# Two-block transformer kernel: halves at the four seams, six modulation sums from two-part accumulators, earlier division of attention's rows

## What is computed

```python
mod = c @ w_ada[l] + b_ada[l]          # first block; the second uses silu(c)
shift_m, scale_m, gate_m, shift_f, scale_f, gate_f = jnp.split(mod, 6, axis=-1)
h = modulate(rms_norm(x, g_pre_mix[l]), shift_m, scale_m)
y_a = sliding_window_attention(q_a, k_a, v_a, attn_sinks[l])
merged = sigmoid(g_a) * (y_a @ w_branch_attn[l]) + sigmoid(g_m) * (y_m @ w_branch_mlstm[l])
x = x + gate_m * rms_norm(merged @ w_out[l], g_post_mix[l])
h2 = modulate(rms_norm(x, g_pre_ffn[l]), shift_f, scale_f)
x = x + gate_f * rms_norm((silu(h2 @ w_gate) * (h2 @ w_up)) @ w_down, g_post_ffn[l])
# the second block: layer norms, a gMLP and an RWKV mixer, and a feed-forward of the same shape
```

## Time and profile before

| | |
|---|---|
| median of three runs | 795.09 us |
| profiled execution | 793.67 us |
| its span | 791.8 us, so 1.9 us lie around it |
| TensorE (PE) busy | 761.5 us, 96% |
| VectorE (DVE) busy | 615.4 us, 78% |
| ScalarE (ACT) busy | 375.9 us, 47% |
| chain that ended last | PE 71%, DVE 20%, DMA 4%, issue 3%, ACT 2% |
| read from HBM | 171.60 MB, 218 GB/s over the span |

### The profile page before, as it was taken

How to read it: one execution, slowest core, us unless ns; L and a number is a source line. 1 busy time by engine, 2 the same in 40 slices (tenths; PEclk the granted TensorE clock), 3 DMA queues, 4 the chain that set the end, 5 groups by cost and what they waited for, 6 DMA issues and landing times.

```text
span 791.8 us, 15369 instructions
## 1 busy us (share of the span) xinstructions
PE 761.5 (96%) x6380; PEld 675.7 (85%) x6380; DVE 615.4 (78%) x813; ACT 375.9 (47%) x553; POOL 41.4 (5%) x61
## 2 busy tenths in 40 slices
PE   4999999989999999999999999999899999999996
PEld 3798899989768999998876987989675999999874
DVE  5869989988978888887868899786697788556457
ACT  3367743744354544453345696432225444454340
POOL 0124000000000000000001000040010000000000
PEclk9999999999999999999999999999999999999998
DMA  9997867764668899988992644301673399666621
GB/s 342 319 318 223 296 213 221 246 227 129 199 230 309 291 351 322 343 303 302 371 334 61 204 128 138 108 4 46 202 236 105 114 315 319 187 189 199 195 83 53
DMA packets 98067, 173.65 MB, mean 219 GB/s; under 512 B 7767, under 2 KB 55230, under 8 KB 97998
## 3 DMA queue, kind: packets, MB, share of 16 engines
q1 hardware_dynamic: 95678, 166.62, 62.8%
q0 software_dynamic: 1872, 5.86, 2.6%
q10 hardware_dynamic: 448, 0.19, 0.1%
HBM read 171.60 MB, written 1.05 MB: 218 GB/s over the span
## 4 chain that ended last, share of the span: by engine, by line
PE 71%; DVE 20%; DMA 4%; issue 3%; ACT 2%; DVEq 0%; SPq 0%; ACTq 0%
PE bank L2246 12%; PE bank L2247 12%; PE bank L2248 12%; PE bank L2302 5%; PE bank L2566 5%; PE bank L2567 5%; PE bank L2568 5%; DVE wlo L498 3%; DVE acc L525 3%; DMA raw<-in_w_ada 2%; PE bank L2722 2%; DVE arena L1365 1%; PE bank L2223 1%; PE bank L2164 1%; PE bank L2225 1%
## 5 line engine op out<-in xcount | busy, mean ns | idle before, releaser
L498 DVE TENSOR_TENSOR wlo<-raw,whi 128x1024 fp32r<-128x1024 f32 (+1 forms) x200 | 239.7, 1213 | 83.2 <-ACT whi L735 80.0
L735 ACT ACTIVATE whi<-raw 128x1024 fp32r<-128x1024 f32 (+1 forms) x200 | 207.2, 1051 | 200.6 <-PE bank L2248 76.2
L2246 PE MATMUL bank<-hh,whi 128*128 128x256 f32 x952 | 267.2, 281 | 0.5 <-DVE wlo L498 0.4
L2247 PE MATMUL bank<-hl,whi 128*128 128x256 f32 x952 | 263.7, 277 | 0.0
L2248 PE MATMUL bank<-hh,wlo 128*128 128x256 f32 x952 | 263.7, 277 | 0.0
L2246 PEld LDWEIGHTS bank<-hh,whi 128*128 128x128 f32 x952 | 178.8, 188 | 3.8 <-issue 2.8
L2247 PEld LDWEIGHTS bank<-hl,whi 128*128 128x128 f32 x952 | 178.8, 188 | 1.2 <-issue 1.2
L2248 PEld LDWEIGHTS bank<-hh,wlo 128*128 128x128 f32 x952 | 179.3, 188 | 0.0
L2566 PE MATMUL bank<-whi,ffh 128*128 128x512 f32 x168 | 65.7, 391 | 0.9 <-DVE wlo L498 0.9
L2567 PE MATMUL bank<-wlo,ffh 128*128 128x512 f32 x168 | 65.4, 389 | 0.0
L2568 PE MATMUL bank<-whi,ffl 128*128 128x512 f32 x168 | 65.4, 389 | 0.0
(11 more groups left out here) (464 smaller groups left out, 1097.4 us busy)
## 6 DMA issues: line engine op xcount, KB each, us to landing
raw<-in_w_ada SPq DMA_DIRECT2D x96, 512.0 KB, 5.3
raw<-in_w_in SPq DMA_DIRECT2D x50, 512.0 KB, 5.0
raw<-in_w_ffn_in SPq DMA_DIRECT2D x80, 256.0 KB, 4.2
raw<-in_w_ffn_down SPq DMA_DIRECT2D x22, 512.0 KB, 5.3
raw<-in_w_ffn_out SPq DMA_DIRECT2D x22, 512.0 KB, 4.2
raw<-in_w_ffn_gate SPq DMA_DIRECT2D x40, 256.0 KB, 4.4
raw<-in_w_ffn_up SPq DMA_DIRECT2D x40, 256.0 KB, 5.7
raw<-in_w_out SPq DMA_DIRECT2D x16, 512.0 KB, 4.1
```

The costliest lines, as they stand in the source:

```text
L498: eng.tensor_tensor(lo[:, 0:nk * width], raw[:, b % RAW, 0:nk * width], hi[:, 0:nk * width].bitcast(fp), ALU.subtract)\
L735: act.activation(weight_place(g)[0][:, 0:nk * width], raw[:, b % RAW, 0:nk * width], ACT.Copy)\
L2246: mm(o, wh[:, k, c], xh[:, kk_, :], start=first, stop=False)
L2247: mm(o, wh[:, k, c], xl[:, kk_, :], start=False, stop=False)
```

## The change

Three things, independent of each other.

1. Where normalised rows are written (`xn` at seam 1, `xt` at seams 2 and 3), each instruction of 1024 columns becomes two of 512, each with its own signal. `turn_rows` waits for the first before its first four transposes and for the second before its last four.
2. For the parts 5, 6, 7, 8, 9 and 11, VectorE behind the eighth block writes a rounded copy of the accumulator (`sum_hi`, a TENSOR_SCALAR of 128x1024 to fp32r) and then the rest in place (`sum_lo`, a TENSOR_TENSOR). `part(d)` sums the two by fp32r matmuls: four instead of two in fp32 for a gate, sixteen instead of eight for the others. Rounded ones are written once for each gate and once for the rest.
3. Attention's second half is divided before the last head's statistics, both `split_ya` follow each other with no `wlo` between them, and 14 of the unread bf16 matmuls stand ahead of `ba0`.

```diff
+        SPLIT_SUMS = {5: 4, 6: 6, 7: 8, 8: 10, 9: 12, 11: 15}
...
                     eng.scalar_tensor_tensor(to, x, by, to, ALU.mult, ALU.add)\
                        .then_inc(sem(f"{me}_blocks"), 1)
+                    if k == 7 and d in SPLIT_SUMS:
+
+                        one, hi, lo = part_split(d)
+                        if d in GATES:
+                            eng.tensor_scalar(one, C("ones"), 1.0, None, ALU.mult).then_inc(sem("sum_split"), 1)
+                        if d == 5:
+                            eng.tensor_scalar(part_split(6)[0], C("ones")[:, 0:SUM_N], 1.0, None, ALU.mult)\
+                               .then_inc(sem("sum_split"), 1)
+                        eng.wait_ge(sem(f"{me}_blocks"), count)
+                        if 6 <= d <= 9:
+                            eng.wait_ge(sem("piece_done"), {6: 6, 7: 6, 8: 8, 9: 7}[d])
+                        eng.tensor_scalar(hi, to, 1.0, None, ALU.mult).then_inc(sem("sum_split"), 1)
+                        eng.wait_ge(sem("sum_split"), SPLIT_SUMS[d] - 1)
+                        eng.tensor_tensor(lo, to, hi.bitcast(fp), ALU.subtract).then_inc(sem("sum_split"), 1)
...
+                    if amid and h == HM - 1:
+                        amid()
...
             take_inter(0)
             divided(0)
-            head_stats(0)
+            head_stats(0, lambda: divided(1))
             head_var(0)
-            divided(1)
             split_ya(0)
+            split_ya(1)
             prepare("ba1", slice(0, 1))
-            split_ya(1)
...
-                TS(xn[:, m * D:(m + 1) * D], xt[:, m, :], st[:, 4 + m:5 + m], None, ALU.mult)\
-                    .then_inc(sem("xn_ready"), 1)
+                for h in range(2):
+                    c = slice(512 * h, 512 * h + 512)
+                    TS(xn[:, D * m + 512 * h:D * m + 512 * h + 512], xt[:, m, c], st[:, 4 + m:5 + m], None, ALU.mult)\
+                        .then_inc(sem("xn_ready"), 1)
...
+                if d in SPLIT_SUMS:
+
+                    one, hi, lo = part_split(d)
+                    pe.wait_ge(sem("sum_split"), SPLIT_SUMS[d])
+                    if d in GATES:
+                        for h in range(2):
+                            c = slice(512 * h, 512 * h + 512)
+                            mm(bank[at + h][:, :], one, hi[:, c], start=True, stop=False)
+                            last = mm(bank[at + h][:, :], one, lo[:, c], start=False, stop=True)
+                    else:
+                        x = 8 * SUM_N * (d == 9)
+                        for t in range(8):
+                            o, c = bank[at][:, x + SUM_N * t:x + SUM_N * t + SUM_N], slice(t * P, t * P + P)
+                            mm(o, hi[:, c], one, start=True, stop=False)
+                            last = mm(o, lo[:, c], one, start=False, stop=True)
+                    last.then_inc(sem("piece_done"), 1)
+                    return
...
             turn_ya(1)
+            run_on(7, 0)
             pe.wait_ge(sem("ya_split"), 2)
             features_out("ba0", four, (yah, yal))
```

More of the change, by code:

```diff
@@ L205, in build @@
         wlo = ctx.enter_context(nc.sbuf_tensor("wlo", [P, HL, SLOT], fr))
+        acc_at = -(-nc.sbuf_base // 32) * 32
         acc = sb("acc", [P, D])
+        pos_acc = [(acc_at - arena_at) // 4]
         xt = sb("xt", [P, MT, D])
@@ L468, in part_acc, with part_split @@
             return hx[:, 4:8, :].rearrange("p t n -> p (t n)") if d == 1 else acc[:, :]
+        SPLIT_SUMS = {5: 4, 6: 6, 7: 8, 8: 10, 9: 12, 11: 15}
+        def part_split(d):
+            sums = 2 * FT * S + 2048
+            at = {5: sums + 4 * D, 6: ARENA - 2048, 7: ARENA - 1024, 8: sums + D, 9: sums, 11: sums + 4 * D}[d]
+            own = pos_acc[0] if d in GATES else sums + D * (d - 6)
+            one = rounded("ones128", ARENA - P, [P]) if d in GATES else rounded("ones32", sums + 5 * D, [SUM_N])
+            return one[:, :], rounded(f"sum_hi{d}", at, [D])[:, :], rounded(f"sum_lo{d}", own, [D])[:, :]
         def turned_h(u, k):
@@ L668, in _ @@
             gate_bias(10)
-            pool.wait_ge(sem("xhat_ready"), 2)
+            pool.wait_ge(sem("xhat_ready"), 4)
             pool.dma_start(lup[0:64, :], A["w_up_2"][0]).then_inc(sem("lora_in"), 16)
@@ L1555, in _, with head_stats @@
             den = st[:, 136:144]
-            def head_stats(m):
+            def head_stats(m, amid=None):
                 dve.wait_ge(sem("inter_used"), 2 * m + 2)
@@ L1780, in ln_rows @@
                 step(dve.reciprocal(st[:, 126 + m:127 + m], st[:, 126 + m:127 + m]))
-                TS(xt[:, m, :], xt[:, m, :], lnmv[:, m, 0:1], st[:, 126 + m:127 + m], ALU.subtract, ALU.mult)\
-                    .then_inc(sem("xhat_ready"), 1)
+                for h in range(2):
+                    c = slice(512 * h, 512 * h + 512)
+                    TS(xt[:, m, c], xt[:, m, c], lnmv[:, m, 0:1], st[:, 126 + m:127 + m], ALU.subtract, ALU.mult)\
+                        .then_inc(sem("xhat_ready"), 1)
             def ln_affine(u, g, b):
@@ L2274, in turn_rows @@
             def turn_rows(u, m):
-                if u == 1:
-                    pe.wait_ge(sem("xn_ready"), 3 + m)
-                    src = xn[:, m * D:(m + 1) * D]
-                else:
-                    pe.wait_ge(sem("xhat_ready"), 2 * u - 3 + m)
-                    src = xt[:, m, :]
-                for k in range(KT):
+                src = xn[:, m * D:(m + 1) * D] if u == 1 else xt[:, m, :]
+                for k in range(KT):
+                    if k % 4 == 0:
+                        if u == 1:
+                            pe.wait_ge(sem("xn_ready"), 3 + 2 * m + k // 4)
+                        else:
+                            pe.wait_ge(sem("xhat_ready"), 4 * u - 7 + 2 * m + k // 4)
                     last = tr(turned_h(u, k), src[:, k * P:(k + 1) * P], ident)
```

## The result

| | before | changed |
|---|---|---|
| median | 795.22 us | 800.6 us (20 runs each) |
| ratio of the two | | 1.0071, 95% interval 1.0056 to 1.0087 |
| profiled execution | 793.67 us, span 791.8 | 801.04 us, span 799.2 |
| TensorE busy | 761.5 us | 767.3 us |
| mean granted clock of the runs | 0.992 | 0.991 |

The account below looks back on a forecast made before the run. TensorE, in flight for 96% of the span, was taken as the bound. Terms -2.4 - 0.26 + 0.19 + 1.16 + 1.0 - 0.81 = -1.1 us took the median from 795.09 to 794.0, range 790.0 to 797.5.

Parts of the forecast that it names:

- attention's new order: Attention's end: dividing earlier lets ba0 start at 174.00 in place of 175.13, -1.13 us.
- the gates' matmuls: Sums of parts 5 and 11: four fp32r products at 0.23 replace four fp32 records at 0.43, -0.81 us each.
- the narrow sums' 0: Narrow sums on TensorE: as many 128x128 loads as before, fp32r at 188 ns, so 0 change.
- seam 3's +0.19: Seam 3: two half instructions cost VectorE 1.0 against about 0.8 for one, so +0.19 us.
- sum_lo`'s 1.22: Split sums on VectorE: sum_lo, a TENSOR_TENSOR like wlo, takes 1.22 us.
- Seam 1: Seam 1: the first half of the rows is ready earlier, so transposes start 0.26 us earlier, -0.26.
- the item starts 2.28 - 1.12 = +1.16 later: Behind part 5: the split delays the next wlo by 2.28 us against a lead of 1.12, costing +1.16 us.
- "+1.0" behind part 6: Behind part 6: a 2.04 us split against 0.98 us of lead left, costing about +1.0 us.
- +1.35 together: All six split sums: +1.16 behind part 5, +1.0 behind part 6, -0.81 at part 11.
- whole -1.7: Attention's end: 14 unread bf16 matmuls fill the pause and keep the granted clock, saving 1.7 us.
- -1.13 + 0.43 = -0.7: Attention's end without the clock's share: ba0 1.13 us earlier, less a 0.43 us wait ahead of turn_ym.
- Splits too dear: Rival at the split sums: a split costs 2.9 us, parts 5, 6 and 7 wait, 796.3 us; chance 0.15.

Follow-up runs that it names:

- dve6_long: Kernel before, with VectorE also writing a rounded copy and three differences, read by nobody (4.5 us), behind part 6's last block: ratio 1.0052.
- att: Kernel before with attention's edit alone (earlier division, adjacent split_ya, 14 unread bf16 matmuls): ratio 0.9993.
- att_norun: Kernel before with attention's edit but without the 14 bf16 matmuls ahead of the first branch product: ratio 0.9986.
- att_halves: Kernel before with attention's edit but without the 14 bf16 matmuls, plus the halves at the seams, no part split: ratio 0.9979.
- best: Kernel before with attention's edit without the 14 bf16 matmuls, the halves at the seams, and only part 11 split: ratio 0.9990.
- sums_no5: Kernel before with parts 6, 7, 8, 9 and 11 split and part 5 left in fp32: ratio 1.0043.

## Why the prediction was wrong

- **The question was put right.** An edit pays if it takes a wait or work from TensorE, and VectorE's splits are paid at the next `wlo` that comes too late. The terms for attention's new order (-1.13 forecast, `ba0` 1.2 sooner), the gates' matmuls, the narrow sums' 0, seam 3's +0.19 and `sum_lo`'s 1.22 were all within 0.1 us in the trace. Seam 1 gave 0.07 in place of 0.26.
- **The step that failed is the price of a wait.** The prediction has "the item starts 2.28 - 1.12 = +1.16 later" and "+1.0" behind part 6, and books a late `wlo` as its length. The waits were even shorter: 1.3 and 0.8 us in all in the changed kernel's two traces, in place of 2.0 and 1.0, since VectorE had more lead than the one trace of before showed. But behind them the chain ran at 117.8 in place of 113.3 ns up to its next interruption, 478 or 766 products, 2.2 or 3.4 us. `dve6_long` measured 4.3 us for a wait of 1.8. The sums were forecast at +1.35 together and cost +5.0 ± 0.5.
- **The rows to see it were there.** The trace of before holds both paces: 632 to 668 runs at 117.8 ns behind a wait of 0.37 us. I had read spacings from one stretch only. What those rows could not tell is which waits would be followed by the worse pace, and that is still open.
- **The clock term was mis-sized.** The "whole -1.7" at attention's end comes from one trace. Over the runs the order gains 0.5 ± 0.3 us by the clock. With -1.13 + 0.43 = -0.7 for the rest, the place would be -1.2; att, att_norun, att_halves and best measured 0.0, -0.8, -1.3 and -0.6 with both parts together.
- **The range was too narrow for it.** None of the rivals had a cost that grows with the length of what follows. "Splits too dear" ended on the right side at 796.3, by a mechanism (2.9 us for a split) that did not happen: a split took 1.9, and 2.1 with its ones.
- **Two terms nobody had.** The kernels with all four narrow splits lost about 2 thousandths of clock more, 1.5 us. And the wait for code at 560 was 2.69 and 2.97 us in the two traces of the changed kernel, 2.27 in `sums_no5`, and 0.50 to 1.72 in the other 17. With the fillers alone (att) it was 0.78, so the fillers move it and in that trace did not lengthen it; what does is open.

The chance of 0.94 for within 1% holds: the change is 0.7% slower.

## What to carry to other kernels

A late operand in front of a long chain of matmuls can cost more than the wait, so before adding work to the engine that feeds the chain, compare it with the lead at each place where the chain could be interrupted, counting lateness that is carried over from the place before. Read the distance between starts in several stretches of the trace of before; if there are two at the same clock, take the difference times the matmuls up to the next interruption as the upper bound of what a new wait adds to its length (here 7 of 11 new waits added it). A loss of clock, or a pace, seen in one trace is one draw: book its mean over executions, not what the trace in hand shows, and take the clock's share out of timed runs before comparing edits of a few tenths of a per cent.

## What the runs showed of the hardware that I had not expected

- The chain of three fp32r products of 256 columns has two steady paces at a granted clock of 1.00, 113.3 and 117.8 ns from start to start, held for up to 766 matmuls and changed only at interruptions. In the stretch of this change 7 of 11 waits were followed by the slower one and none of the 11 traces without a wait had it.
- One thousandth of lost clock goes with 0.77 us of 795, closely enough that taking it out halves the spread of the timed runs.
- TensorE stood still for 0.5 to 3.0 us at a fixed place in its code, in a loop where it starts some 36 matmuls in a microsecond (145 in 4 us), in every trace, and went on 1.25 to 1.51 us after a 16 KB packet of code had landed.
- fp32r weights of 128x128 load in 187 to 192 ns even for 32 moving columns, as fp32 ones do.
